# Last products by column halves in a hybrid decoder block with a mixture of experts

## The chip, the cores and the metric

The kernel runs on one core of one Trainium2 chip. The number is the device time of one execution in microseconds, as the median of several runs. The engines are TensorE (PE, with its weight loads shown as PEld), VectorE (DVE), ScalarE (ACT), GpSimd (POOL) and SyncE (SP), which issues most transfers. TensorE writes to PSUM, eight banks of 128 partitions by 512 float32 columns; everything else lies in SBUF or DRAM.

## The reference, cut to what matters

One layer: 512 tokens of 1024 features, a mixer (retention and dilated attention), then a mixture of experts with 4 of 32 experts for each token, and a last RMS norm.

```python
x = x + hybrid_mixer(rms_norm(x, norm_mix_g), w_in, w_out, pos)
...
logits = ht @ w_router + b_router
top_val, top_idx = lax.top_k(logits, TOP_K)          # 4 of 32
gates = softmax(top_val)
...
gu = xb @ w_gu + b_gu                                # 1024 -> 2048, one expert's rows
act = x_glu * sigmoid(1.702 * x_glu) * (x_lin + 1.0) # both clamped at 7
y[token] += gate * (act @ w_dn + b_dn)               # 1024 -> 1024
...
x = x + y
return x * rsqrt(mean(x * x, axis=-1) + 1e-5) * norm_final_g
```

The change concerns the last lines: the share of the last expert and of all down biases is added to x, and the final norm is taken.

## The kernel before

The 512 tokens lie as four chunks (`NC = 4`) of 128 rows; a row has 1024 columns, in two halves of `UW = 512`, since a PSUM bank holds 512. Each engine has its own written program; the order on an engine is the order of the code, and engines wait for each other through semaphores. There is no scheduler.

The experts run one after the other. For each, up to 128 rows of its tokens are gathered, multiplied with weights that stream in from DRAM (each float32 product is made of three products of a high and a low part), and the result is added to `acc_rows` in DRAM by a scatter. The residual x is in `acc_rows` too. The last expert is different: its result never goes through DRAM. ScalarE and VectorE split it by column halves into `y_hi` and `y_lo` (lines 1039 to 1042 and 1501 to 1506). Meanwhile, when the scatter of the expert before it is complete, SyncE loads the four chunks of `acc_rows` back into `x1` (line 520, one transfer of 512 KB for each chunk, semaphores `x_in[0]` to `x_in[3]`).

Then TensorE does what lines 2082 to 2093 say: for each chunk c and each half it adds three products in one PSUM bank: the gates times the down biases (`gateT`, `bdn`), and a matrix of zeros and ones that puts the expert's rows at their tokens (`hasT`) times `y_hi` and times `y_lo`. These are 4 x 2 x 3 = 24 products, all on line 2075. Chunk c uses banks `LAST_BANK[c]` and the one behind it, so 0 and 1, 2 and 3, 6 and 7, 4 and 5. The last expert's own result stands in banks 4 and 5, which is why chunk 3 waits for `y_lo`. After both halves of a chunk, `f_ps` goes up by one (it stands at 1 before, from line 2000).

Behind that, for each chunk:

- VectorE adds both banks to `x1` (`final_sum`, line 1545), waiting for the chunk's load and for `f_ps`, and signals `f_sum`.
- ScalarE squares the chunk and accumulates each row's sum of squares (`final_square`, line 1068), signals `f_sq`. The profile shows the write of the accumulator as an instruction of its own, ACTIVATION_READ_ACCUMULATOR.
- GpSimd multiplies chunks 0 and 1 by the gain (line 733).

With all four sums of squares, ScalarE takes the root (line 1081) beside VectorE's half variance (line 1553); four small VectorE steps on 128x4 numbers make the reciprocal root with one correction (lines 1556 to 1559); ScalarE scales chunks 0 and 1 (line 1075), VectorE chunks 2 and 3 (line 1562), and SyncE stores the four chunks (lines 543 and 545). Between the split and the last products every engine reads whether any expert had more rows than 128 and branches around the code for that case, which is not taken here.

Of the kernel before, what the change touches and what calls it, by code (L numbers as in the profile page):

```python
# [65 lines left out]
LAST_BANK = [0, 2, 6, 4]  # L66

# [88 lines left out]
def build(nc, x, norm_mix_g, w_in, w_out, norm_ffn_g, w_router, b_router,  # L156
# [299 lines left out]
    with block as block:  # L456
# [92 lines left out]
        def _(pl):  # L549
# [181 lines left out]
            for c in range(2):  # L731
                pl.wait_ge(f_sum, c + 1)
                nc.gpsimd.tensor_tensor(with_gain[:, c, :], x1[:, c, :], gain_row[:, :], ALU.mult).then_inc(f_gain, 1)

        @block.scalar
        def _(act_e):
# [328 lines left out]
            def final_square(c):  # L1065

                act_e.wait_ge(f_sum, c + 1)
                nc.scalar.activation((y, lin, sig, square_out)[c][:, :], x1[:, c, :], ACT.Square,
                                     accum_out=small[:, 10, c:c + 1]).then_inc(f_sq, 1)
# [8 lines left out]
            for c in range(NC):  # L1078
                final_square(c)
            act_e.wait_ge(f_sq, NC)  # L1080
# [6 lines left out]
        def _(v):  # L1087
# [453 lines left out]
            def final_sum(c):  # L1541

                v.wait_ge(x_in[c], 32)
                v.wait_ge(f_ps, c + 2)
                nc.vector.tensor_tensor(x1[:, c, :], x1[:, c, :], ps[:, LAST_BANK[c]:LAST_BANK[c] + 2, :].rearrange("p b t -> p (b t)"),
                                        ALU.add).then_inc(f_sum, 1)

            v.wait_ge(fin_g_in, 16)
            for c in range(NC):
                final_sum(c)  # L1550
            v.wait_ge(f_sq, NC)
            half_var, root, step, rstd = (small[:, k, 0:NC] for k in (11, 12, 13, 3))
            nc.vector.tensor_scalar(half_var, small[:, 10, 0:NC], -0.5 / D, -0.5 * EPS, ALU.mult, ALU.add).then_inc(f_var, 1)
            v.wait_ge(f_var, 1)
# [11 lines left out]
        def _(pe):  # L1566
# [515 lines left out]
            for c in range(NC):  # L2082
                for half in range(2):
                    if c == NC - 1:
                        pe.wait_ge(ylo_s, half + 1)
                    last_half(c, half, gateT, bdn, True, False)
                    if c == 0:
                        pe.wait_ge(yhi_s, half + 2)
                    last_half(c, half, hasT, y_hi, False, False)
                    if c == 0:  # L2090
                        pe.wait_ge(ylo_s, half + 1)
                    last = last_half(c, half, hasT, y_lo, False, True)
                last.then_inc(f_ps, 1)
# [22 lines left out]
```

## Time and profile before

| | |
|---|---|
| Median of 3 runs | 1419.56 us (1418.79 to 1420.21) |
| Span of the profiled execution | 1416.6 us |
| TensorE busy in it | 1389.3 us (98%), granted clock 0.996 |
| VectorE, ScalarE, GpSimd busy | 1246.5, 1055.2, 402.8 us |
| First of the last products, by the trace | 1398.3 us |
| First store issued | 1409.66 us |

The span runs from the first to the last instruction of one execution; the runs' time has some 3 us more around it. The experts fill almost the whole of it. All that the change touches lies in the last 20 us. Times in the rows below are counted from the span's start. A bracket at the end of a row says how long the engine had been idle before it, and what ended that. A row with x2 or x4 merges neighbours: its length runs from the first's start to the last's end.

### The profile page before, as it was taken

To read this page: it belongs to the slowest core of one execution; us is meant where nothing else is said; L and a number is where in the kernel's file an instruction comes from. 1 tells how busy PE (TensorE), PEld (TensorE's weight loads), DVE (VectorE), ACT (ScalarE), POOL (GpSimd) and SP (SyncE) were. 2 spreads that over 40 slices of the span, in tenths; PEclk is the share of its full clock that TensorE was granted. 3 is DMA by queue.
4 is the path that set the end of the run, shared out by engine and by line. 5 is a ranking of instruction groups with operands and counts; after the bars stand their busy time and mean duration, and the time that the engine had idled before them with its cause. 6 is when DMAs were issued, how large, how long until landed. Compare 5 with 4: busy or idle time off the path is not lost.

```text
span 1416.6 us, 19760 instructions
## 1 busy us (share of the span) xinstructions
PE 1389.3 (98%) x6583; PEld 1154.8 (82%) x6583; DVE 1246.5 (88%) x959; ACT 1055.2 (74%) x779; POOL 402.8 (28%) x233
## 2 busy tenths in 40 slices
PE   7999999999999999999999999999999999999996
PEld 6877888878888888888888888888888888888884
DVE  5534647499999999999999999999999999999996
ACT  5234334488888888888888888888888888888875
POOL 0000001067433333333333333333333333333332
PEclk9999999999999999999999999999999999999998
DMA  8311423389999999999999999999999999999993
GB/s 312 106 38 60 134 75 123 124 305 367 385 388 383 382 380 383 379 380 374 380 378 384 375 382 381 380 378 383 382 379 382 383 387 381 383 383 381 383 358 131
DMA packets 80135, 453.73 MB, mean 320 GB/s; under 512 B 12825, under 2 KB 13089, under 8 KB 31852
## 3 DMA queue, kind: packets, MB, share of 16 engines
q1 hardware_dynamic: 68968, 432.55, 77.5%
q0 software_dynamic: 10016, 17.44, 4.8%
q10 hardware_dynamic: 1124, 3.38, 0.7%
q8 instruction: 17, 0.28, 0.1%
q14 instruction: 10, 0.08, 0.0%
HBM read 447.60 MB, written 22.59 MB: 332 GB/s over the span
## 4 chain that ended last, share of the span: by engine, by line
PE 93%; DVE 4%; ACT 2%; DMA 1%; issue 1%; DVEq 0%; ACTq 0%
PE ps L1947 16%; PE ps L1952 16%; PE ps L1948 16%; PE ps L1905 8%; PE ps L1907 8%; PE ps L1913 8%; PE ps L1583 4%; PE ps L1584 4%; PE ps L1591 4%; PE ps L1896 2%; PE ps L1883 2%; DVE wlo L1103 1%; PE ps L1686 1%; DVE wlo L1112 1%; PE ps L1717 1%; PE ps L1667 1%
## 5 line engine op out<-in xcount | busy, mean ns | idle before, releaser
L1947 PE MATMUL ps<-whi,xT_hi 128*128 128x512 f32 x992 | 389.4, 393 | 1.7 <-ACT ps L959 1.0
L1948 PE MATMUL ps<-whi,xT_lo 128*128 128x512 f32 x992 | 386.1, 389 | 0.0
L1112 DVE TENSOR_TENSOR wlo<-raw,whi 128x2048 fp32r<-128x2048 f32 x138 | 315.9, 2293 | 45.6 <-ACT whi L752 45.3
L752 ACT ACTIVATE whi<-raw 128x2048 fp32r<-128x2048 f32 x138 | 264.9, 1920 | 90.2 <-PE ps L1952 71.3
L1108 DVE SCALAR_TENSOR_TENSOR wlo<-raw,gffn,whi 128x2048 fp32r<-128x2048 f32 x124 | 311.0, 2551 | 0.9
L1952 PE MATMUL ps<-wlo,xT_hi 128*128 128x512 f32 x992 | 265.6, 389 | 0.0
L750 ACT ACTIVATE whi<-raw,gffn 128x2048 fp32r<-128x2048 f32 x124 | 245.5, 2004 | 9.9 <-PE ps L1952 9.9
L1947 PEld LDWEIGHTS ps<-whi,xT_hi 128*128 128x128 f32 x992 | 186.4, 188 | 40.6 <-ACT ps L959 1.4
L1952 PEld LDWEIGHTS ps<-wlo,xT_hi 128*128 128x128 f32 x992 | 186.2, 188 | 38.6
L1948 PEld LDWEIGHTS ps<-whi,xT_lo 128*128 128x128 f32 x992 | 186.4, 188 | 37.7
L1905 PE MATMUL ps<-whi,actT_hi 128*128 128x512 f32 x496 | 195.9, 395 | 0.0
L1907 PE MATMUL ps<-whi,actT_lo 128*128 128x512 f32 x496 | 193.2, 390 | 0.0
L1108 DVE SCALAR_TENSOR_TENSOR wlo<-raw_b,gffn,whi 128x2048 fp32r<-128x2048 f32 x62 | 147.1, 2373 | 0.0
L1108 DVE SCALAR_TENSOR_TENSOR wlo<-raw_a,gffn,whi 128x2048 fp32r<-128x2048 f32 x62 | 145.2, 2342 | 0.0
L750 ACT ACTIVATE whi<-raw_a,gffn 128x2048 fp32r<-128x2048 f32 x62 | 124.6, 2010 | 22.0 <-PE ps L1952 22.0
L750 ACT ACTIVATE whi<-raw_b,gffn 128x2048 fp32r<-128x2048 f32 x62 | 124.5, 2008 | 21.9 <-PE ps L1952 21.9
L1913 PE MATMUL ps<-wlo,actT_hi 128*128 128x512 f32 x496 | 132.7, 389 | 0.0
L627 POOL COPY idx_scatter<-tab 128x1 uint32 (+1 forms) x31 | 50.6, 1632 | 286.1 <-ACT y L940 286.0
L627 POOL COPY idx_gather<-tab 128x1 uint32 (+1 forms) x30 | 13.5, 449 | 336.6 <-PE ps L1883 334.2
L1913 PEld LDWEIGHTS ps<-wlo,actT_hi 128*128 128x128 f32 x496 | 93.1, 188 | 19.7
L1907 PEld LDWEIGHTS ps<-whi,actT_lo 128*128 128x128 f32 x496 | 93.2, 188 | 18.4
L1905 PEld LDWEIGHTS ps<-whi,actT_hi 128*128 128x128 f32 x496 | 93.2, 188 | 18.3
(269 smaller groups left out, 1926.2 us busy)
## 6 DMA issues: line engine op xcount, KB each, us to landing
raw<-in_w_gate_up SPq DMA_DIRECT2D x130, 1024.0 KB, 8.6
raw<-in_w_down SPq DMA_DIRECT2D x126, 1024.0 KB, 9.1
raw_a<-in_w_gate_up SPq DMA_DIRECT2D x63, 1024.0 KB, 7.5
raw_b<-in_w_gate_up SPq DMA_DIRECT2D x63, 1024.0 KB, 8.0
raw<-in_w_in SPq DMA_DIRECT2D x14, 1024.0 KB, 5.2
raw<-in_w_out SPq DMA_DIRECT2D x4, 1024.0 KB, 5.0
x<-in_x SPq DMA_DIRECT2D x4, 512.0 KB, 7.4
acc_rows<-x SPq DMA_DIRECT2D x4, 512.0 KB, 5.3
```

What stands on the lines that cost most here:

```text
L627: return nc.gpsimd.tensor_copy(index[:, 0:1], tab[:, bass.ds(e, 1), 0].bitcast(U32))
L750: nc.scalar.activation(whi_slot(n), raw_slot(slot_of(n)), ACT.Copy, scale=gffn_of(n)).then_inc(hi_done, 1)
L752: nc.scalar.activation(whi_slot(n), raw_slot(slot_of(n)), ACT.Copy).then_inc(hi_done, 1)
L1108: nc.vector.scalar_tensor_tensor(out=wlo_slot(n), in0=raw_slot(slot_of(n)), scalar=gffn_of(n), in1=whi_slot(n).bitcast(F32), op0=ALU.mult, ...
L1112: nc.vector.tensor_tensor(wlo_slot(n), raw_slot(slot_of(n)), whi_slot(n).bitcast(F32), ALU.subtract).then_inc(lo_done, 1)
L1583: mm(out_ap, x_hi_of(k), w_hi_ap, start=opened and k == 0, stop=False)
L1905: mm(ps[:, bank + half, :], x_hi_t[:, k0 + k, :], w_hi_ap, start=k0 + k == 0 and not started, stop=False, skip_group_check=started)
L1907: mm(ps[:, bank + half, :], x_lo_t[:, k0 + k, :], w_hi_ap, start=False, stop=False, skip_group_check=started)
L1913: last = mm(ps[:, bank + half, :], x_hi_t[:, k0 + k, :], w_lo_ap, start=False, stop=k0 + k == KD - 1, skip_group_check=started)
L1947: mm(ps[:, part, :], xT_hi[:, u, :], w_hi_ap, start=False, stop=False, skip_group_check=True)
L1948: mm(ps[:, part, :], xT_lo[:, u, :], w_hi_ap, start=False, stop=False, skip_group_check=True)
L1952: last = mm(ps[:, part, :], xT_hi[:, u, :], w_lo_ap, start=False, stop=u == U_GU - 1, skip_group_check=True)
```

## The change

`LAST_HALVES` sets a new order of eight pieces, each a chunk and a column half: left halves of chunks 0, 1, 2, right halves of 0, 1, 2, then both halves of chunk 3. TensorE makes its three products for one piece after the other and signals `f_ps` after each. VectorE's sums, ScalarE's squares, `f_sum` and `f_sq` go by pieces in the same order. A row now has two sums of squares, in columns 0 to 3 and 4 to 7 of `small[:, 10]`; VectorE adds them in one more instruction of 128x4, for which the root and the half variance wait. GpSimd waits for a chunk's right half. Scalings and stores stay whole chunks.

```diff
--- before.py
+++ after.py
@@ -64,6 +64,7 @@
 U_ALL = U_MOE + E * U_E
 NOVER = 15
 LAST_BANK = [0, 2, 6, 4]
+LAST_HALVES = [(0, 0), (1, 0), (2, 0), (0, 1), (1, 1), (2, 1), (3, 0), (3, 1)]
 
 
 C_ID = 0
@@ -729,7 +730,7 @@
 
             pl.wait_ge(fin_g_in, 16)
             for c in range(2):
-                pl.wait_ge(f_sum, c + 1)
+                pl.wait_ge(f_sum, LAST_HALVES.index((c, 1)) + 1)
                 nc.gpsimd.tensor_tensor(with_gain[:, c, :], x1[:, c, :], gain_row[:, :], ALU.mult).then_inc(f_gain, 1)
 
         @block.scalar
@@ -1062,11 +1063,13 @@
 
             nc.scalar.activation(small[:, 12, 0:1], cst[:, C_ONE:C_ONE + 1], ACT.Sqrt)
 
-            def final_square(c):
-
-                act_e.wait_ge(f_sum, c + 1)
-                nc.scalar.activation((y, lin, sig, square_out)[c][:, :], x1[:, c, :], ACT.Square,
-                                     accum_out=small[:, 10, c:c + 1]).then_inc(f_sq, 1)
+            def final_square(k):
+
+                c, half = LAST_HALVES[k]
+                piece = slice(half * UW, (half + 1) * UW)
+                act_e.wait_ge(f_sum, k + 1)
+                nc.scalar.activation((y, lin, sig, square_out)[c][:, piece], x1[:, c, piece], ACT.Square,
+                                     accum_out=small[:, 10, half * NC + c:half * NC + c + 1]).then_inc(f_sq, 1)
 
             def final_scale(c):
 
@@ -1075,9 +1078,9 @@
                 nc.scalar.activation(with_gain[:, c, :], with_gain[:, c, :], ACT.Copy,
                                      scale=small[:, 3, c:c + 1]).then_inc(hn_s, 1)
 
-            for c in range(NC):
-                final_square(c)
-            act_e.wait_ge(f_sq, NC)
+            for k in range(2 * NC):
+                final_square(k)
+            act_e.wait_ge(f_var, 1)
             nc.scalar.activation(small[:, 12, 0:NC], small[:, 10, 0:NC], ACT.Sqrt, scale=1.0 / D,
                                  bias=cst[:, C_EPS:C_EPS + 1]).then_inc(f_root, 1)
             final_scale(0)
@@ -1538,20 +1541,23 @@
                                                     ALU.add).then_inc(v_add, 1)
 
 
-            def final_sum(c):
-
+            def final_sum(k):
+
+                c, half = LAST_HALVES[k]
+                piece = x1[:, c, half * UW:(half + 1) * UW]
                 v.wait_ge(x_in[c], 32)
-                v.wait_ge(f_ps, c + 2)
-                nc.vector.tensor_tensor(x1[:, c, :], x1[:, c, :], ps[:, LAST_BANK[c]:LAST_BANK[c] + 2, :].rearrange("p b t -> p (b t)"),
-                                        ALU.add).then_inc(f_sum, 1)
+                v.wait_ge(f_ps, k + 2)
+                nc.vector.tensor_tensor(piece, piece, ps[:, LAST_BANK[c] + half, :], ALU.add).then_inc(f_sum, 1)
 
             v.wait_ge(fin_g_in, 16)
-            for c in range(NC):
-                final_sum(c)
-            v.wait_ge(f_sq, NC)
+            for k in range(2 * NC):
+                final_sum(k)
+            v.wait_ge(f_sq, 2 * NC)
             half_var, root, step, rstd = (small[:, k, 0:NC] for k in (11, 12, 13, 3))
+            nc.vector.tensor_tensor(small[:, 10, 0:NC], small[:, 10, 0:NC], small[:, 10, NC:2 * NC], ALU.add).then_inc(f_var, 1)
+            v.wait_ge(f_var, 1)
             nc.vector.tensor_scalar(half_var, small[:, 10, 0:NC], -0.5 / D, -0.5 * EPS, ALU.mult, ALU.add).then_inc(f_var, 1)
-            v.wait_ge(f_var, 1)
+            v.wait_ge(f_var, 2)
             v.wait_ge(f_root, 1)
             link(nc.vector.reciprocal(root, root))
             link(nc.vector.tensor_tensor(step, root, root, ALU.mult))
@@ -2079,18 +2085,16 @@
             pe.wait_ge(bdn_s, 1)
             pe.wait_ge(bdn_zero, 1)
             pe.wait_ge(hasT_s, 1)
-            for c in range(NC):
-                for half in range(2):
-                    if c == NC - 1:
-                        pe.wait_ge(ylo_s, half + 1)
-                    last_half(c, half, gateT, bdn, True, False)
-                    if c == 0:
-                        pe.wait_ge(yhi_s, half + 2)
-                    last_half(c, half, hasT, y_hi, False, False)
-                    if c == 0:
-                        pe.wait_ge(ylo_s, half + 1)
-                    last = last_half(c, half, hasT, y_lo, False, True)
-                last.then_inc(f_ps, 1)
+            for c, half in LAST_HALVES:
+                if c == NC - 1:
+                    pe.wait_ge(ylo_s, half + 1)
+                last_half(c, half, gateT, bdn, True, False)
+                if c == 0:
+                    pe.wait_ge(yhi_s, half + 2)
+                last_half(c, half, hasT, y_hi, False, False)
+                if c == 0:
+                    pe.wait_ge(ylo_s, half + 1)
+                last_half(c, half, hasT, y_lo, False, True).then_inc(f_ps, 1)
 
 
 _INS = ["x", "norm_mix_g", "w_in", "w_out", "norm_ffn_g", "w_router", "b_router",
```

TensorE, the last products: first as they stood, then as they stand now. Three rows are one piece. The name `last_halves_read` is the semaphore of `y_hi`, `last_y_lo` that of `y_lo`.

```order
L2075 MATMUL ps<-bdn,gateT 128x512 [waits down_bias_cleared,hasT_ready,down_bias_ready,gateT_lo_ready]
L2075 MATMUL ps<-y_hi,hasT 128x512 [waits last_halves_read]
L2075 MATMUL ps<-y_lo,hasT 128x512 [waits last_y_lo]
L2075 MATMUL ps<-bdn,gateT 128x512
L2075 MATMUL ps<-y_hi,hasT 128x512 [waits last_halves_read]
L2075 MATMUL ps<-y_lo,hasT 128x512 [waits last_y_lo]
L2075 MATMUL ps<-bdn,gateT 128x512
```

```order
L2081 MATMUL ps<-y_hi,hasT 128x512 [waits last_halves_read]
L2081 MATMUL ps<-y_lo,hasT 128x512 [waits last_y_lo]
L2081 MATMUL ps<-bdn,gateT 128x512
L2081 MATMUL ps<-y_hi,hasT 128x512
L2081 MATMUL ps<-y_lo,hasT 128x512
L2081 MATMUL ps<-bdn,gateT 128x512
L2081 MATMUL ps<-y_hi,hasT 128x512
L2081 MATMUL ps<-y_lo,hasT 128x512
L2081 MATMUL ps<-bdn,gateT 128x512
L2081 MATMUL ps<-y_hi,hasT 128x512 [waits last_halves_read]
L2081 MATMUL ps<-y_lo,hasT 128x512 [waits last_y_lo]
```

Between the pair of waits for the left half of `y` and the pair for the right half there was one product, the first of the second piece; now there are seven.

VectorE, the sums and the steps behind them, before and now. `last_rows_summed` is `f_ps`, `x_in0` to `x_in3` are the loads of the chunks.

```order
L1545 TENSOR_TENSOR x_52<-x_52,ps 128x1024 [waits last_rows_summed,x_in0,final_gain_in]
L1545 TENSOR_TENSOR x_52<-x_52,ps 128x1024 [waits last_rows_summed,x_in1]
L1545 TENSOR_TENSOR x_52<-x_52,ps 128x1024 [waits last_rows_summed,x_in2]
L1545 TENSOR_TENSOR x_52<-x_52,ps 128x1024 [waits last_rows_summed,x_in3]
L1553 TENSOR_SCALAR small<-small 128x4 [waits final_squares]
L1556 RECIPROCAL small<-small 128x4 [waits final_root,final_variance]
```

```order
L1550 TENSOR_TENSOR x_52<-x_52,ps 128x512 [waits last_rows_summed,x_in0,final_gain_in]
L1550 TENSOR_TENSOR x_52<-x_52,ps 128x512 [waits last_rows_summed,x_in1]
L1550 TENSOR_TENSOR x_52<-x_52,ps 128x512 [waits last_rows_summed,x_in2]
L1550 TENSOR_TENSOR x_52<-x_52,ps 128x512 [waits last_rows_summed,x_in0]
L1550 TENSOR_TENSOR x_52<-x_52,ps 128x512 [waits last_rows_summed,x_in1]
L1550 TENSOR_TENSOR x_52<-x_52,ps 128x512 [waits last_rows_summed,x_in2]
L1550 TENSOR_TENSOR x_52<-x_52,ps 128x512 [waits last_rows_summed,x_in3] x2
L1557 TENSOR_TENSOR small<-small 128x4 [waits final_squares]
L1559 TENSOR_SCALAR small<-small 128x4 [waits final_variance]
L1562 RECIPROCAL small<-small 128x4 [waits final_root,final_variance]
```

The wait for the load of chunk 2 stood in front of the third of four whole sums, and stands in front of the third of eight half sums. The new addition stands between the squares and the half variance.

## Rows read from the trace of the kernel before

**Rows 1.** The chain that ended last, late part: start us, us, what.
```profile
1399.85 4.84 PE ps L2075 x20
...
1404.78 1.23 DVE x L1545
...
1406.03 1.16 ACT square_out L1068 x2
...
1407.22 0.31 ACT small L1081
```

**Rows 2.** Instructions in order of time, VectorE: start us, us, line, what.
```profile
1401.01 1.22 DVE L1545 TENSOR_TENSOR x<-x,ps 128x1024 f32<-128x1024 f32 x1 [0.99 <-DMA x<-acc_rows]
...
1402.15 1.21 DVE L1545 TENSOR_TENSOR x<-x,ps 128x1024 f32<-128x1024 f32 x1
...
1403.42 1.22 DVE L1545 TENSOR_TENSOR x<-x,ps 128x1024 f32<-128x1024 f32 x1
```

**Rows 3.** The same view, the queue of SyncE: loads of chunks 0 to 3.
```profile
1396.20 0.33 SPq L520 DMA_DIRECT2D x<-acc_rows  x1
...
1396.58 0.43 SPq L520 DMA_DIRECT2D x<-acc_rows  x1
...
1397.05 0.43 SPq L520 DMA_DIRECT2D x<-acc_rows  x1
...
1397.53 1.28 SPq L520 DMA_DIRECT2D x<-acc_rows  x1
```

**Rows 4.** Line L520: load 0; loads 0, 1; loads 1, 2; all four.
```profile
DMA to landing us min/median/max: 4.5/4.5/4.5
...
DMA to landing us min/median/max: 4.5/4.9/5.3
...
DMA to landing us min/median/max: 5.3/5.8/6.3
...
DMA to landing us min/median/max: 4.5/5.8/7.0
```

**Rows 5.** Busy time by stretch: stretch, length, busy by engine, PEclk, DMA share, GB/s.
```profile
1403.25:1403.50 0.25, 0.25 (x3) 0.21 (x2) 0.20 (x2) 0.25 (x3) 0.25 (x1) 1.00 0.04 16
```

**Rows 6.** DMA queues from 1397.5 to 1398: kind: packets, MB, share.
```profile
q8 instruction: 1, 0.02, 11.6%
```

**Rows 7.** Instructions in order of time, weight loads and VectorE: waits for y_lo.
```profile
1398.77 0.19 PEld L2075 LDWEIGHTS ps<-y_lo,hasT 128*128 128x128 f32 x1 [0.23 <-DVE y_lo L1504]
...
1399.27 0.75 DVE L1504 SCALAR_TENSOR_TENSOR y_lo<-ps,tab,y_hi 128x512 fp32r<-128x512 f32 x1 [0.55 <-ACT y_hi L1041]
...
1400.07 0.19 PEld L2075 LDWEIGHTS ps<-y_lo,hasT 128*128 128x128 f32 x1 [0.60 <-DVE y_lo L1504]
```

**Rows 8.** The same view, VectorE at 240 us: two half sums.
```profile
240.50 1.29 DVE L1285 TENSOR_TENSOR x<-x,ps 128x512 f32<-128x512 f32 x2
```

**Rows 9.** The same view, ScalarE: one square's read, the next square.
```profile
1403.24 0.18 ACT L1068 ACTIVATION_READ_ACCUMULATOR y<-x 128x1 f32 x1
...
1403.40 1.07 ACT L1068 ACTIVATE lin<-x 128x1024 f32<-128x1024 f32 x1
```

**Rows 10.** The same view, ScalarE at 249 us: a square of 512 columns.
```profile
248.95 0.62 ACT L877 ACTIVATE squares<-x 128x512 f32<-128x512 f32 x1
...
249.47 0.19 ACT L877 ACTIVATION_READ_ACCUMULATOR squares<-x 128x1 f32 x1
```

**Rows 11.** The same view, VectorE: small steps.
```profile
1407.83 0.16 DVE L1557 TENSOR_TENSOR small<-small 128x4 f32<-128x4 f32 x1
...
1408.03 0.16 DVE L1558 TENSOR_TENSOR small<-small 128x4 f32<-128x4 f32 x1
```

**Rows 12.** The same view, GpSimd and ScalarE: products with the gain, scalings.
```profile
1402.39 4.73 POOL L733 TENSOR_TENSOR with_gain<-x,gain_row 128x1024 f32<-128x1024 f32 x2 [9.81 <-DVE x L1545]
...
1408.48 2.19 ACT L1075 ACTIVATE with_gain<-with_gain,small 128x1024 f32<-128x1024 f32 x2 [0.96 <-DVE small L1559]
```

**Rows 13.** Busy time by stretch, as in rows 5: the stores.
```profile
1409.65:1416.50 6.85, 0.00 (x0) 0.00 (x0) 1.25 (x2) 1.02 (x1) 0.00 (x0) 0.50 0.77 306
```

## The prediction

> **What bounds the kernel now.** I read the chain of waits first [rows 1]. Behind the last expert it is TensorE's 24 last products, ending at 1404.68, then VectorE's sum of chunk 3, ScalarE's square of chunk 3, a root on four numbers, four small VectorE steps and the scaling. The stores follow. So the change sits on the chain of the last 20 us and touches nothing ahead of it: the span up to 1396 is the same program.
>
> The chain names TensorE, and here the reader has to look at who else was ready at the same moment. The four sums begin at 1401.01, 1402.15, 1403.42 [rows 2] and 1404.78 [rows 1], each 1.21 to 1.22 long. So VectorE is all but full: 5.00 us hold four sums of 4.88 in all. TensorE holds back the last two by 0.06 and 0.14 at most. A faster TensorE alone would give 0.2 us.
>
> The third party is the rows themselves. A sum adds products to a chunk that SyncE loads back from DRAM. The four loads are issued at 1396.20, 1396.58, 1397.05 and 1397.53 [rows 3]. They take 4.5, 5.3, 6.3 and 7.0 us to land [rows 4]; these rows are for the first load alone, the first two, the middle two and all four, and each maximum is the latest load's. That is 1400.7, 1401.9, 1403.35 and 1404.5. Each sum starts within 0.1 to 0.35 us of its own load's landing. Before the change loads and sums march in step, one chunk every 1.3 us, so the loads hide. One reason for the late landings shows: the 16 DMA engines together move only 16 GB/s from 1403.25 on, while load 3 is not there before 1404.5 [rows 5], so a few stragglers land last, and one fetch of instructions sits in the same queues at 1397.5 (11.6% of 16 engines over 0.5 us, so 0.93 us of one engine) [rows 6].
>
> **The change part by part.** I number the eight pieces in the new order: left halves of chunks 0, 1, 2, right halves of 0, 1, 2, then left and right of 3.
>
> TensorE keeps its 24 products. Before, it waited 0.23 us for the left y_lo, and 0.60 us for the right one inside chunk 0, which is complete at 1400.02 [rows 7]. In the new order six products (6 x 0.24 = 1.4 us; 20 took 4.84 [rows 1]) stand in front of the right half's waits, and TensorE arrives at them at about 1400.5, behind 1400.02. It gains some 0.7 us and ends at about 1404.0. That is a real gain, but nothing waits for it as long as VectorE or a load is later.
>
> VectorE gets eight sums of 128x512 for four of 128x1024. Two of just this kind, same tile and PSUM, took 1.29 us together [rows 8] against 1.21 to 1.22 for one whole: a half alone is 0.69, and back to back they stand 0.60 apart. Eight cost 7 x 0.60 + 0.69 = 4.9 us if nothing holds them: no gain and no loss. But the order of the loads they need is now 0, 1, 2, 0, 1, 2, 3, 3. The third piece needs chunk 2 after only two half sums of work. Piece 1 starts at 1401.01 as before and ends at 1401.70. Piece 2 waits for load 1 and runs 1402.1 to 1402.8. Piece 3 waits for load 2 and starts at 1403.42, where chunk 2's whole sum started, and ends at 1404.11. At that time the old order had two chunks summed and was well into the third; the new one has three halves, 1.5 chunks. Behind piece 3, in order on VectorE, stand pieces 4 to 6, whose data were there long ago, and 7 and 8. They run back to back: piece 8 starts at 1403.42 + 5 x 0.605 = 1406.44 and ends at 1407.13, against 1406.01 before.
>
> This is also the place to weigh the Trainium skill. The row shows overlap between neighbours (1.29 for two of 0.69). The Trainium skill, page VectorE: DVE Perf Modes, section on the TRN2 errata, says that memory latency is exposed between instructions and many small tiles pay it each; read strictly, pieces would stand 0.69 apart and piece 8 would end at 1407.56. ScalarE would then end about 0.1 us later than in my sum, so both readings lie in my range; the row is what I take.
>
> ScalarE gets eight squares for four, with eight reads of the accumulator. One whole: the next square stands 0.16 us behind the start of the read [rows 9]. A 512 wide one of an earlier stage has its read 0.52 behind its own start, and the read takes 0.19 [rows 10]. So halves stand 0.68 apart, and they are slower than VectorE's 0.60: ScalarE becomes the one that ends last. Square 3 starts at 1404.13, 0.02 behind its sum; square 8 at 1404.13 + 5 x 0.68 = 1407.53; its number is there at 1407.53 + 0.52 + 0.19 = 1408.24. Before it was 1406.03 + 1.16 = 1407.19 [rows 1]. That is **+1.05 us**. The intended saving (half a last square, 0.45 us) is in this sum already.
>
> The joining addition has the size of the small steps, which stand 0.20 apart [rows 11]. Before, root and half variance started together at 1407.22, and only the root was on the chain. Now the root waits for the addition, and crosses from VectorE to ScalarE: 0.20, at most 0.28. **+0.2 us**. The half variance, one more small step of 0.16, still hides beside the root (0.31).
>
> GpSimd multiplies chunks 0 and 1 by the gain, 4.73 us for both [rows 12]. It may start chunk 0 when piece 4 is summed (1404.7 instead of 1402.25) and ends at 1409.6. ScalarE scales both products in 2.19 us from 1408.48 on [rows 12], so it takes up the second at about 1409.6, and everything later by 1.25 at 1410.8 after. The cover of the second product shrinks from 2.4 to 1.2 us and is still there. Cost nothing; if a product took 0.6 us more each, it would begin to show.
>
> The stores leave from 1409.65 on and fill the DMA at 306 GB/s to the end [rows 13]: a shift of the scaling goes to the end one to one.
>
> Sum: 1.05 + 0.2 = +1.25 us. Span 1416.6 + 1.25 = 1417.8. The median of the runs is 1419.56, 3.0 us above the span; with the same surroundings the forecast is **1420.8 us**, 0.09% slower, which counts as no change: about 0.2% (2.84 us) is what a measurement of this kernel can tell, and the three runs before lie 1.4 us apart.
>
> **Rivals.** (A) *The loads are on time.* If the stragglers do not come in another build or execution, load 2 lands nearer to 1402, VectorE is never held, and ScalarE sets the end: square 1 at 1401.72 + 7 x 0.68 = 1406.48, done at 1407.19. That is exactly the old time, the addition makes it +0.2; if the first sum too starts up to 0.4 us earlier, -0.2. So 1419.4 to 1419.8. For it: the straggling is some 1.3 us behind the bulk. Against: all four landings of this trace show it, and the loads and the code ahead of them are unchanged. Chance 0.17.
>
> (B) *The saving comes as meant*, since TensorE is the bound that the chain names: TensorE earlier by 0.7 and last square shorter by 0.45, less 0.2 for the addition, gives -0.95: 1418.6. Against it: VectorE was full and had at most 0.2 us from TensorE. Chance 0.04; even this is within 0.2%.
>
> (C) *Slower than measurable: instructions come late.* VectorE and ScalarE have a dozen more instructions in the tail. If this moves the end of a fetched block into the squares while the loads fill the queues, the engine stands for a fetch: 0.93 us of one DMA engine [rows 6], behind loads that are up to 1.4 us late. 1.25 + 2.3 = +3.6: 1423.1. It decides from 1.6 us of standing on. The Trainium skill, Runtime: NRT & Kernel Launch, section Instruction fetch mechanics, says that crossing a block is mostly hidden; no run here shows a crossing in the tail. Chance 0.04.
>
> (D) *GpSimd's cover is gone*: products slower beside VectorE's halves, +1.3 to +2.5 us, 1421 to 1422. Before, both products ran beside VectorE's sums at 2.4 us each, so 0.04. That the program doesn't do what it says is excluded by the order of its instructions; 0.
>
> **The numbers.** Forecast 0.71 (1420.3 to 1421.4: the addition 0.2 to 0.28, piece spacing 0.60 to 0.69, landing of load 2 give or take 0.3), A 0.17, B 0.04, C 0.04, D 0.04. Predicted 1420.8. The range takes in A and D's lower part, with half a microsecond of the median's own scatter: 1419.2 to 1421.9. Chances: faster by over 0.2% 0.01, slower by over 0.2% 0.04, within 0.95.
>
> **What would show it.** Right: TensorE ends at about 1404.0; the third sum waits for a DMA landing, with VectorE idle about 0.4 and 0.6 us ahead of pieces 2 and 3; sums 4 to 8 without gaps; squares 0.68 apart without waits from the third on; root some 0.2 us behind the addition; stores leaving at 1410.9. Wrong: load 2 landing before 1402.3, idle time of ScalarE between the late squares, GpSimd waited for by a scaling, or any difference ahead of 1396.

## The result and the profile after

| | before | changed |
|---|---|---|
| Median of 21 runs each, in turn on one chip | 1418.91 us | 1420.95 us |
| Lowest and highest | 1416.8, 1421.84 | 1418.97, 1422.88 |
| Span of the profiled execution | 1416.6 us | 1418.1 us |
| Ratio | | 1.0015, 95% interval 1.0009 to 1.0020 |

The changed kernel is 2.1 us slower by the ratio (1.3 to 2.8). That is inside the forecast range; 21 runs tell it from no difference, and the upper end of the interval just reaches the 0.2% that was set as the limit. But the forecast sum was 1.25 us, and the trace shows that what lies behind the measured number is in good part something else than the reason given. In the traces the place of the tail in the span shifts by up to 3 us with what happened before it, so I count from two marks: the first sum of x, and the start of VectorE's second `y_lo`.

The late part of the chain of waits of the changed kernel (start, length in us, what):

```profile
1396.21 6.30 DMA x<-acc_rows
1402.52 0.02 issue
1402.54 0.70 DVE x L1550
1403.23 0.02 issue
1403.26 0.72 ACT sig L1071 x2
...
1405.82 1.23 ACT square_out L1071 x4
1407.05 0.02 issue
1407.08 1.61 DVE small L1557
1408.68 0.03 issue
1408.71 0.30 ACT small L1084
```

TensorE has left the chain [rows 1]. It now begins with the load of chunk 2, as forecast, and goes on through the squares. Then stands something that was not forecast at all: the joining addition, four numbers per row, takes 1.61 us. The same stretch in order of time, VectorE, ScalarE and GpSimd:

```profile
1400.34 0.69 DVE L1550 TENSOR_TENSOR x<-x,ps 128x512 f32<-128x512 f32 x1 [1.00 <-DMA x<-acc_rows]
1401.21 0.69 DVE L1550 TENSOR_TENSOR x<-x,ps 128x512 f32<-128x512 f32 x1 [0.18 <-DMA x<-acc_rows]
1402.54 3.68 DVE L1550 TENSOR_TENSOR x<-x,ps 128x512 f32<-128x512 f32 x6 [0.64 <-DMA x<-acc_rows]
...
1403.98 4.67 POOL L734 TENSOR_TENSOR with_gain<-x,gain_row 128x1024 f32<-128x1024 f32 x2 [12.08 <-DVE x L1550]
...
1404.50 0.61 ACT L1071 ACTIVATE lin<-x 128x512 f32<-128x512 f32 x1
1405.02 0.18 ACT L1071 ACTIVATION_READ_ACCUMULATOR lin<-x 128x1 f32 x1
1405.12 0.61 ACT L1071 ACTIVATE sig<-x 128x512 f32<-128x512 f32 x1
...
1407.08 1.60 DVE L1557 TENSOR_TENSOR small<-small 128x4 f32<-128x4 f32 x1 [0.86 <-ACT square_out L1071]
1408.71 0.17 DVE L1559 TENSOR_SCALAR small<-small 128x4 f32<-128x4 f32 x1
```

Three readings. The sums [rows 2] stand much as forecast: held 0.18 and 0.64 us by the loads of chunks 1 and 2, then six in 3.68 us without a gap. The squares are 0.62 apart, not 0.68. And the addition ends at 1408.68, just behind GpSimd's second product, which ends at 1403.98 + 4.67 = 1408.65. Before, that product ended at 1402.39 + 4.73 = 1407.12 [rows 12], and VectorE's first small step began at 1407.22, 0.1 us later: the program had a deadline there that no wait in it expresses and no bracket shows.

The bracket of the first sum names the load of chunk 0. But in eight of the thirteen traces here, these two among them, the first sum starts 1.74 or 1.75 us behind the start of the second `y_lo`, while the load lands 0.1 to 0.4 us ahead of it. What stands there is then more likely VectorE's own way through the branch; no run tests it. The third sum starts 0.03 us behind the landing of its load (1396.21 + 6.30 = 1402.51).

From the first sum: the root started 6.21 us behind it before and 8.37 behind it now. Of these 2.16 us, 0.53 lie ahead of the addition (square 8 complete 6.71 behind the first sum, against 6.18), and 1.63 are the addition.

### The profile page after: what moved, and what is told of

The parts are those of the page before. It is cut to its first block, busy times and chain, and to the rows that moved or that the text cites. A ratio compares the mean times of both kernels' runs of the same rounds, so it can differ in the third digit from the quotient of the medians.

```text
span 1418.1 us, 19777 instructions
## 1 busy us (share of the span) xinstructions
PE 1388.6 (98%) x6583; PEld 1154.3 (81%) x6583; DVE 1248.3 (88%) x964; ACT 1055.2 (74%) x787; POOL 402.3 (28%) x233
## 4 chain that ended last, share of the span: by engine, by line
PE 92%; DVE 3%; DMA 2%; ACT 2%; issue 1%; DVEq 0%; ACTq 0%; SPq 0%; POOLq 0%
PE ps L1953 16%; PE ps L1958 16%; PE ps L1954 16%; PE ps L1911 8%; PE ps L1913 8%; PE ps L1919 8%; PE ps L1589 4%; PE ps L1590 4%; PE ps L1597 4%; PE ps L1902 2%; PE ps L1889 2%; DVE wlo L1106 1%; PE ps L1692 1%; PE ps L1723 1%; PE ps L1673 1%
```

## The experiments

Theory S: a VectorE instruction that needs what GpSimd is using to reach SBUF stands until GpSimd's instruction is done, and the new order moved GpSimd's products into VectorE's small steps. What the runs can show is who stands and until when; that the way to SBUF is the reason stays theory. Rivals: the joining step is dear by itself (J); only the hold by the load of chunk 2 counts (L).

All times of one comparison come from the same chip. The last two columns are the start of VectorE's scaling in the one profiled execution, counted from the start of the second `y_lo` and from the first sum. They differ by what the first sum waited; in e1, e5 and e8 to e10 that was TensorE.

| kernel | ratio to before, 95% interval | scaling behind y_lo | behind the first sum |
|---|---|---|---|
| before | 1 | 9.15 us | 7.41 us |
| changed | 1.0015, 1.0009 to 1.0020 | 11.32 | 9.57 |
| e1, before with GpSimd late | 1.0013, 1.0004 to 1.0022 | 11.76 | 9.58 |
| e2, changed, no products with the gain | 1.0004, 0.9995 to 1.0013 | 10.07 | 8.32 |
| e3, changed, chunk order | 0.9999, 0.9990 to 1.0008 | 9.31 | 7.56 |
| e4, changed, join by reduction | 1.0012, 1.0003 to 1.0021 | 11.04 | 9.29 |
| e5, only chunk 3 halved | 1.0001, 0.9992 to 1.0010 | 10.43 | 7.75 |
| e6, changed, products in quarters | 1.0013, 1.0004 to 1.0022 | 11.24 | 9.49 |
| e7, changed, two chunks then two | 1.0003, 0.9994 to 1.0012 | 10.25 | 8.50 |
| e8, before, stream shifted | 1.0003, 0.9993 to 1.0012 | 13.11 | 7.89 |
| e9, changed, stream shifted | 1.0019, 1.0010 to 1.0028 | 11.44 | 9.41 |
| e10, e5, stream shifted | 1.0011, 1.0002 to 1.0021 | 10.35 | 7.74 |
| e11, changed, products by pieces | 1.0000, 0.9990 to 1.0009 | 10.09 | 8.34 |

**e1: GpSimd late in the kernel before.**

```diff
-                pl.wait_ge(f_sum, c + 1)
+                pl.wait_ge(f_sum, c + 3)
```

> The kernel before, with one number changed: GpSimd's two products with the gain wait for the third and the fourth whole sum instead of the first and the second. Sums, squares, root and VectorE's small steps are those of before. Theory S (shared access to SBUF): a VectorE instruction whose two operands both lie in SBUF stands until GpSimd's product is done. The products then run from about 1404.8 to 1409.5, the square of the root (line 1557, 0.16 us before, at 1407.8) lasts until the second product ends, so 1.5 to 1.7 us, half variance and reciprocal (one operand) stay at 0.17 and 0.18, and the end is 1.4 to 1.6 us later than before (ratio 1.0010 to 1.0011). Rival J (the joining addition itself is dear, as the first reader of the two sets of sums): there is no joining addition here, the step stays 0.16 us, the time that of before.

Measured 1.0013. In order of time:

```profile
1405.24 4.65 POOL L733 TENSOR_TENSOR with_gain<-x,gain_row 128x1024 f32<-128x1024 f32 x2 [12.90 <-DVE x L1545]
...
1407.66 2.26 DVE L1553 TENSOR_SCALAR small<-small 128x4 f32<-128x4 f32 x1 [1.22 <-ACT square_out L1068]
1407.66 0.30 ACT L1081 ACTIVATE small<-small,cst 128x4 f32<-128x4 f32 x1
1409.95 0.18 DVE L1556 RECIPROCAL small<-small 128x4 f32<-128x4 f32 x1
```

No halves, no joining step, one number changed, and from the first sum to the scaling the kernel before now takes 9.58 us, like the changed one (9.57). So J is not needed for a step to stand. The size came out larger than expected (9.58 - 7.41 = 2.2 us in the trace, 0.3 of them sums that waited for TensorE; 1.4 to 1.6 forecast), and the wrong instruction stood. I had expected the half variance to pass, since it has one operand; it took 2.26 us, to 1409.92, when GpSimd ended at 1409.89. So two operands are not the condition.

**e2: no products.** The products of chunks 0 and 1 with the gain are left out, so these rows come out without the gain.

```diff
-            for c in range(2):
-                pl.wait_ge(f_sum, LAST_HALVES.index((c, 1)) + 1)
-                nc.gpsimd.tensor_tensor(with_gain[:, c, :], x1[:, c, :], gain_row[:, :], ALU.mult).then_inc(f_gain, 1)
...
-                act_e.wait_ge(f_gain, c + 1)
...
-                nc.scalar.activation(with_gain[:, c, :], with_gain[:, c, :], ACT.Copy,
+                nc.scalar.activation(with_gain[:, c, :], x1[:, c, :], ACT.Copy,
```

> The changed kernel without GpSimd's products with the gain of chunks 0 and 1: that multiplication is left out, ScalarE scales x1 straight into with_gain. Theory S: the joining addition falls from 1.60 to 0.16-0.20 us, the end lies 1.4 us ahead of the changed kernel, so 0.5 to 0.8 us behind before (ratio 1.0004 to 1.0006). Rival J: the addition stays near 1.6 us and the time stays that of the changed kernel (1.0015).

```profile
1402.63 3.68 DVE L1546 TENSOR_TENSOR x<-x,ps 128x512 f32<-128x512 f32 x6 [0.56 <-DMA x<-acc_rows]
...
1407.18 0.16 DVE L1553 TENSOR_TENSOR small<-small 128x4 f32<-128x4 f32 x1 [0.87 <-ACT square_out L1068]
```

The same addition in the same place takes 0.16 us, so J falls, and 1.0004 is what was expected. The hold by the load stays, 0.56 us.

**e3: chunk order.**

```diff
-LAST_HALVES = [(0, 0), (1, 0), (2, 0), (0, 1), (1, 1), (2, 1), (3, 0), (3, 1)]
+LAST_HALVES = [(0, 0), (0, 1), (1, 0), (1, 1), (2, 0), (2, 1), (3, 0), (3, 1)]
```

> The changed kernel with the list LAST_HALVES in chunk order (left and right of 0, of 1, of 2, of 3); halves, signals and joining addition stay. Theory S with L (the order holds VectorE at the load of chunk 2 and moves GpSimd's start): no idle time of 0.6 us ahead of the third piece, sums end where they ended before, last square about 0.5 us earlier than before relative to the first sum, GpSimd starts after the second piece and ends some 4.8 us later, the addition stands only 0.3-0.5 us for it, and the root starts within 0.1 us of where it did before: the time is that of before (ratio 0.9998 to 1.0002). Rival J: addition 1.6 us, root 1.1 us late, ratio 1.0008. Rival P (VectorE was never held, halving costs by itself): as the changed kernel, 1.0015.

```profile
1400.26 5.37 DVE L1550 TENSOR_TENSOR x<-x,ps 128x512 f32<-128x512 f32 x8 [1.00 <-DMA x<-acc_rows]
...
1401.70 4.74 POOL L734 TENSOR_TENSOR with_gain<-x,gain_row 128x1024 f32<-128x1024 f32 x2 [9.86 <-DVE x L1550]
...
1406.42 0.17 DVE L1557 TENSOR_TENSOR small<-small 128x4 f32<-128x4 f32 x1 [0.79 <-ACT square_out L1071]
```

Halves, signals and joining addition are all there, and the time is that of before. No sum waits for a load behind the first. The eight take 5.37 us, not the 4.9 of VectorE's own pace: they stand 0.67 apart on average, which is about what TensorE needs for three products of 0.23. So the last square is complete 6.13 us behind the first sum (6.18 before), and not 0.5 us sooner as I had expected. GpSimd is through at 1406.44, when the addition starts at 1406.42. So the price of the change lies in the order of the eight pieces, which sets both the hold and GpSimd's start, and not in the halving, which costs 0.15 us here (7.56 against 7.41).

**e4: join with one operand.**

```diff
-            nc.vector.tensor_tensor(small[:, 10, 0:NC], small[:, 10, 0:NC], small[:, 10, NC:2 * NC], ALU.add).then_inc(f_var, 1)
+            nc.vector.tensor_reduce(out=small[:, 14, 0:NC], in_=small[:, 10, 0:2 * NC].rearrange("p (h c) -> p c h", h=2),
+                                    op=ALU.add, axis=AX.X).then_inc(f_var, 1)
```

> The changed kernel with the joining step as a reduction over a 4x2 view, one operand, in place of an addition of two operands. Theory S: the join takes 0.16-0.20 us beside GpSimd's product, then half variance, root and reciprocal run, and now the square of the root (two operands) stands until the second product is done, about 0.5 us. The end lies 0.6-0.7 us ahead of the changed kernel, 1.3-1.5 us behind before (ratio 1.0010). Rival J: the join is dear in any form, 1.6 us, time as changed; or, if only this one addition is dear, the whole 1.4 us come back (ratio 1.0005) and no later step is long.

```profile
1405.72 4.65 POOL L734 TENSOR_TENSOR with_gain<-x,gain_row 128x1024 f32<-128x1024 f32 x2 [12.18 <-DVE x L1550]
...
1408.83 0.16 DVE L1557 TENSOR_REDUCE small<-small 128x4 f32<-128x8 f32 x1 [0.87 <-ACT square_out L1071]
1409.02 1.39 DVE L1560 TENSOR_SCALAR small<-small 128x4 f32<-128x4 f32 x1
```

The reduction passes beside GpSimd in 0.16 us, so a join is not dear in this form. The half variance behind it stands 1.39 us, to 1410.41 (GpSimd: 1410.37). The stand has moved one step back, past the root's start, and the reciprocal behind it on VectorE is late again. Gain against the changed kernel: 0.3 us by either of the last two columns, where I had expected 0.6 to 0.7.

e1 and e4 together give the condition as these traces show it: TENSOR_TENSOR with both operands in SBUF and TENSOR_SCALAR from SBUF to SBUF stand, TENSOR_REDUCE does not, nor do the sums of x with one operand in PSUM, which ran beside GpSimd all along. The Trainium skill, GPSIMD Engine Reference, section Specifications, has this rule: GpSimd's interfaces to SBUF are shared with VectorE, with contention from VectorE instructions that have two SBUF inputs or are in a 2-port performance mode. The traces agree, with 1.60 us for the first kind and 2.26 for TENSOR_SCALAR, if that ran in such a mode, which no row shows.

**e5: only chunk 3 by halves.** Sums and squares of chunks 0 to 2 are whole and the order is by chunk; the two sums of chunk 3's rows are joined by a reduction.

```diff
-LAST_HALVES = [(0, 0), (1, 0), (2, 0), (0, 1), (1, 1), (2, 1), (3, 0), (3, 1)]
+PIECES = [(0, 0, 2), (1, 0, 2), (2, 0, 2), (3, 0, 1), (3, 1, 1)]      # chunk, first half, halves
...
-                pl.wait_ge(f_sum, LAST_HALVES.index((c, 1)) + 1)
+                pl.wait_ge(f_sum, c + 1)
```

> Sums and squares of chunks 0, 1 and 2 whole, in chunk order, as in the kernel before; only chunk 3 by halves; the two sums of its rows are joined by a reduction (one operand, 128x1). GpSimd starts behind chunk 0's whole sum, as before. Theory S (a VectorE instruction that needs the second access to SBUF, by two operands or as TENSOR_SCALAR, stands until GpSimd's running product ends): last square done 0.5 us earlier than before relative to the first sum, join 0.2, root 0.3 us earlier than before; GpSimd's second product ends about 0.1-0.2 us behind the join, so the half variance stands that long, hidden beside the root. End 0.2-0.3 us ahead of before, ratio 0.9997 to 1.0000, which the runs can't tell from 1; in the trace the first small step stands under 0.4 us. Rival T (the stand has another cause, a halved square or a joining step as such): a step of 1.4-1.6 us shows here too, ratio 1.0008.

```profile
1403.15 5.11 DVE L1550 TENSOR_TENSOR x<-x,ps 128x1024 f32<-128x1024 f32 x5 [1.93 <-PE ps L2082]
```

1.0001, and no step stands (reduction 0.15, half variance 0.17): rival T falls. GpSimd was through at 1409.25, 0.26 us ahead of the reduction. The forecast gain did not come: from the first sum to the scaling it takes 7.75 us (7.41 before). Two gaps of 0.12 and 0.14 us between the sums are waits for TensorE, and the first sum itself waited 1.93 us for TensorE; e8 to e10 are on this. The 0.5 us expected of the last square were not there either: ScalarE runs through its last three squares without a gap (1407.10 to 1409.48), so without the waits it would have been some 0.1 us ahead of before (an estimate from its squares of 1.06 and 0.61 us).

**e6: GpSimd's products in quarters.**

```diff
-                nc.gpsimd.tensor_tensor(with_gain[:, c, :], x1[:, c, :], gain_row[:, :], ALU.mult).then_inc(f_gain, 1)
+                for q in range(4):
+                    part = slice(q * 256, (q + 1) * 256)
+                    last = nc.gpsimd.tensor_tensor(with_gain[:, c, part], x1[:, c, part], gain_row[:, part], ALU.mult)
+                last.then_inc(f_gain, 1)
```

> The changed kernel with each of GpSimd's two products with the gain in four instructions of 256 columns (about 0.6 us each) in place of one of 2.4 us; their start and sum are the same. Theory S1 (VectorE stands until the GpSimd instruction that is running ends): the addition stands at most 0.7 us, and each later small step with two operands, and the TENSOR_SCALAR, may stand up to 0.6 us again, until GpSimd is through: the steps are spread, the root starts 0.9-1.5 us earlier than in the changed kernel, the sum of all stands is at most 1.6. Ratio 1.0005 to 1.0012. S2 (VectorE stands until GpSimd has nothing more to do): one stand of 1.4-1.8 us at the addition as in the changed kernel, ratio 1.0015.

```profile
1402.96 5.53 POOL L736 TENSOR_TENSOR with_gain<-x,gain_row 128x256 f32<-128x256 f32 x8 [12.11 <-DVE x L1553]
...
1406.06 0.41 DVE L1560 TENSOR_TENSOR small<-small 128x4 f32<-128x4 f32 x1 [0.87 <-ACT square_out L1074]
1406.50 0.66 DVE L1562 TENSOR_SCALAR small<-small 128x4 f32<-128x4 f32 x1
...
1407.19 0.18 DVE L1565 RECIPROCAL small<-small 128x4 f32<-128x4 f32 x1
1407.40 0.43 DVE L1566 TENSOR_TENSOR small<-small 128x4 f32<-128x4 f32 x1
1407.87 0.65 DVE L1567 TENSOR_TENSOR small<-small 128x4 f32<-128x4 f32 x1
1408.54 0.16 DVE L1568 SCALAR_TENSOR_TENSOR small<-small 128x4 f32<-128x4 f32 x1
```

S1, clearly: VectorE gets in when one GpSimd instruction ends, and stands again at the next step. Four stands make 0.25 + 0.49 + 0.27 + 0.49 = 1.5 us, the products take 5.53 in place of 4.67, and nothing is won. RECIPROCAL passes, like the reduction. Behind GpSimd's end at 1408.49 the last step is 0.16 again.

**e7: two chunks, then two.**

```diff
+LAST_HALVES = [(0, 0), (1, 0), (0, 1), (1, 1), (2, 0), (2, 1), (3, 0), (3, 1)]
```

> The changed kernel with the list in the order left of 0, left of 1, right of 0, right of 1, left and right of 2, left and right of 3. The load of chunk 2 is needed only by the fifth piece, and GpSimd starts behind the third. Theory S: no idle time of VectorE ahead of the third piece by a load; GpSimd starts 1.2 us after the second piece's start plus 0.7, so about 2.0-2.6 us behind the first sum (3.6 in the changed kernel, 1.4 in chunk order), ends 4.7 us later, and the addition, due 6.2-6.3 us behind the first sum, stands 0.4-1.1 us; the end lies 0.6-1.2 us ahead of the changed kernel: ratio 1.0003 to 1.0009, between chunk order (0.9999) and the changed kernel (1.0015). Rival L (the load's hold is the price, GpSimd's start is not): as chunk order, 0.9999, no stand.

```profile
1401.63 4.65 DVE L1550 TENSOR_TENSOR x<-x,ps 128x512 f32<-128x512 f32 x7 [0.39 <-DMA x<-acc_rows]
...
1403.07 4.72 POOL L734 TENSOR_TENSOR with_gain<-x,gain_row 128x1024 f32<-128x1024 f32 x2 [10.95 <-DVE x L1550]
...
1407.07 0.75 DVE L1557 TENSOR_TENSOR small<-small 128x4 f32<-128x4 f32 x1 [0.79 <-ACT square_out L1071]
```

No hold by load 2, and still a stand: 0.75 us, to 1407.82, with GpSimd through at 1407.79. L alone would have shown none. With GpSimd's start 1.4, 2.5 and 3.6 us behind the first sum (e3, e7, changed) the addition takes 0.17, 0.75 and 1.60.

**e11: products by pieces.** The changed kernel, its order untouched; GpSimd's two products become four, and start sooner.

```diff
-            for c in range(2):
-                pl.wait_ge(f_sum, LAST_HALVES.index((c, 1)) + 1)
+            for c, half in ((0, 0), (1, 0), (0, 1), (1, 1)):
+                piece = slice(half * UW, (half + 1) * UW)
+                pl.wait_ge(f_sum, LAST_HALVES.index((c, half)) + 1)
```

> The changed kernel, order and all, with GpSimd's two products with the gain in four of 512 columns, each waiting only for its own piece: left of 0, left of 1, right of 0, right of 1. Theory S: what costs is where GpSimd's work ends, not the order of the pieces as such. The left halves (1.2 us each) run beside pieces 1 to 3, the right halves start behind piece 4 at the soonest, 3.6 us behind the first sum, and end at about 6.0 to 6.2 us behind it; the joining addition is due at 6.7. So it takes 0.16-0.20 us in place of 1.60, the root starts 1.4 us earlier than in the changed kernel and the time is that of the kernel without the products: ratio 1.0003 to 1.0007. Rival: the addition stands although GpSimd is through, or products of 512 columns take over 1.5 us each beside VectorE: ratio 1.0010 or more.

```profile
1404.00 2.53 POOL L735 TENSOR_TENSOR with_gain<-x,gain_row 128x512 f32<-128x512 f32 x2 [0.37 <-DVE x L1553]
...
1407.18 0.16 DVE L1560 TENSOR_TENSOR small<-small 128x4 f32<-128x4 f32 x1 [0.87 <-ACT square_out L1074]
```

GpSimd ends at 1406.53 in place of 1408.65 in the changed kernel, the addition takes 0.16, and the ratio is 1.0000 (0.9990 to 1.0009). Both last columns are 1.2 us below the changed kernel, and 8.34 us is what the kernel without the products has (8.32). The ratio is better than the 1.0003 to 1.0007 expected. But it does not show that the order is free: its interval is 1.3 us wide to either side, and in the traces this order still takes 0.9 us more than before (8.34 against 7.41) and 0.8 more than chunk order (7.56). That is the hold by the loads.

**e8 to e10: TensorE's idle time.** In every trace up to here TensorE stands ahead of the fifth of the last products with no releaser shown: 0.34 us before, 1.21 in the changed kernel, 1.20 in e1, whose TensorE program is that of before. The three kernels have twenty products more in the branch that is not taken:

```diff
             with pe.If(total > 0):
+                pe.wait_ge(hasT_s, 1)
+                for _ in range(20):
+                    nc.tensor.transpose(ps[:, 2, 0:P], has[:, 0, :].bitcast(F32), ident)
```

> The kernel before with twenty more TensorE products in the branch that is not taken, ahead of the last products: nothing more is executed, only the place of what follows in the stream of instructions moves. In every trace so far TensorE stands 0.3 to 1.7 us ahead of the fifth last product with no releaser shown. Theory F: this is a block of instructions that arrives late, its fetch being the one seen among the loads of x; with the border moved off, TensorE has no such idle time, the last product ends 0.3-1.4 us earlier relative to y_lo, VectorE's sums are bound by VectorE and the loads: root 0.2-0.9 us earlier, ratio 0.9993 to 0.9999. If the fetch is also what makes the loads late (F2), the loads land in 3.3 to 5.7 us in place of 4.5 to 7.0. Rival G: the idle time comes from the matrix itself (banks, weights, waits): it stays at the fifth product.

> The changed kernel with the same twenty unexecuted products. F: no idle time ahead of the fifth product; this alone gains nothing, since VectorE waits for loads. F2: the load of chunk 2 lands about 1.3 us earlier relative to its issue, VectorE's idle time ahead of pieces 2 and 3 (0.18 and 0.64 us) falls under 0.2 in all, GpSimd starts and ends about 0.6-0.8 us earlier and the joining addition, 0.3-0.6 earlier, stands 1.3-1.6 us: end 0.5-0.8 us ahead of the changed kernel, ratio 1.0008 to 1.0012. F without F2: 1.0015. Theory S is untouched: the addition still stands to the end of GpSimd's second product.

> Only chunk 3 by halves, as before in this study, with the twenty unexecuted products. F: its first sum waited 1.9 us for TensorE; without the idle time it starts as in the kernel before, root 0.3 us earlier than in the padded kernel before if GpSimd's second product is through by then, else about the same; the half variance may stand up to 0.5 us. Ratio 0.9990 to 0.9997. G: as before padding, 1.0001.

TensorE around the last products, in the changed kernel, then in e8 and in e9:

```profile
1400.04 0.39 PE L2081 MATMUL ps<-y_hi,hasT 128*128 128x512 f32 x1 [1.21 <-issue]
```

```profile
1402.22 0.77 PE L2078 MATMUL ps<-bdn,gateT 128*128 128x512 f32 x1 [2.94 <-issue]
```

```profile
1401.02 0.47 PE L2084 MATMUL ps<-bdn,gateT 128*128 128x512 f32 x1 [1.72 <-issue]
```

The idle time moved, with nothing executed that was not executed before: from the fifth product to the first, in all three. Rival G falls, it belongs to the place in the stream of instructions. But the gain that F forecast did not come: what TensorE waits for is not sooner there, it is needed four products sooner. The kernels are no faster (1.0003, 1.0019, 1.0011; the intervals of the last two lie above 1, and for e10 its trace, much like e5's, gives no reason).

What it waits for can be narrowed down. One fetch of 16 KB on queue 8 runs among the loads of x in every one of the thirteen traces; in e5 from 1400 to 1401 the queues hold

```profile
q8 instruction: 1, 0.02, 5.8%
```

The times of its packet, and of TensorE's next product behind the idle time, in us:

| | fetch ends | TensorE goes on | between | idle |
|---|---|---|---|---|
| before | 1398.43 | 1399.85 | 1.42 | 0.34 |
| changed | 1398.74 | 1400.04 | 1.30 | 1.21 |
| e5 | 1400.99 | 1402.40 | 1.41 | 1.69 |
| e8 | 1400.50 | 1402.22 | 1.72 | 2.94 |
| e9 | 1399.29 | 1401.02 | 1.73 | 1.72 |

In the ten kernels without the twenty products the distance is 1.25 to 1.53 us, in the three with them 1.72 to 1.73, while the idle time itself goes from 0.34 to 2.94: it is as long as the fetch is late. That speaks for F. A releaser is shown in no trace, and what makes the fetch late stays open.

In e8's profiled execution, the slowest of its 11 (1423.09 us), the 2.94 us had a second price. The granted clock was 1.00 (2.4 GHz) until then, and 0.50 (1.2 GHz) behind it, here from 1402.5 to 1405:

```profile
1402.50:1405.00 2.50, 2.50 (x7) 1.92 (x7) 0.00 (x0) 0.00 (x0) 0.00 (x0) 0.50 0.39 154
```

Products started 0.43 us apart in that stretch (1402.79, 1403.21) and 0.23 from 1405.6 on, at 1.00 again. So the first sum waited 4.47 us for TensorE. The median of the 11 runs is 0.2 us below that of before, so one execution must differ much from another here. Behind the 1.72 us of e9 the clock stayed at 1.00.

F2 is not borne out, and not excluded: load 0 landed in 3.2 and 3.4 us in e5 and e8, where the fetch came latest, and in 4.5 to 4.8 elsewhere, but the slowest load took 7.0 to 7.2 us in every trace, and the hold by load 2 is still 0.63 us in e9. In e9 the addition stands 1.60 us again.

## Why the prediction was right or wrong

*TensorE is not the bound.* Right in what followed, wrong in its number: I had it end at 1404.0, 0.7 us sooner. It ended at 1404.34 + 0.39 = 1404.73, which is 6.1 us behind the second `y_lo` where it had been 5.4 (1404.68 - 1399.27): 0.7 us later, since the idle time ahead of its fifth product was 1.21 us. In the changed kernel this is hidden, since the pieces wait for loads.

*The load of chunk 2 holds VectorE.* Right. The load took 6.3 us, as before. I had pieces 2 and 3 wait 0.4 and 0.6 us, the trace has 0.18 and 0.64; piece 3 starts 2.20 us behind the first sum (2.41 forecast), and the rest runs through in 3.68 (3.71). In chunk order the hold is gone (e3).

*ScalarE's squares, +1.05.* The mechanism was right, the size was twice the real one: +0.53. Of the 0.52 too much, 0.21 is that piece 3 started sooner than forecast, and 0.31 is the spacing of the five squares behind it. The spacing of 0.68 had a term of 0.16 between the read of the accumulator and the next square [rows 9]. That was not ScalarE's own time but a wait: the second sum ended at 1402.15 + 1.21 = 1403.36 [rows 2], and the square began at 1403.40. Where no sum is waited for, the gap is 0.10 (1405.02 to 1405.12), squares are 0.62 apart, and VectorE's 0.60 is nearly as slow. A gap between two instructions is the engine's price only when nothing that the second waits for ends in it.

*The joining addition, +0.2.* This is the step that failed. It kept the root back by 1.63 us: 0.16 for itself (e2, e11), 0.03 to the root, and 1.44 in which it stood for GpSimd's product.

*GpSimd's later start costs nothing.* The same failure seen from the other side. I had compared its end with the next reader of its output, ScalarE's scaling, and found 1.2 us of cover; the forecast end (8.6 us behind the first sum, 8.31 measured) was near enough. But another engine needed not its output but that it be through, 0.1 us behind GpSimd's old end; that this is for its access to SBUF is theory S. Rival D had the right engine, a chance of 0.04 and the wrong direction: it had GpSimd slowed by VectorE. GpSimd's products took 4.67 us beside the halves, 4.73 before; VectorE was the one that stood.

*The sum.* 0.53 + 1.63 = 2.16 by the trace, 2.1 by the runs, 1.25 forecast: an overcharged term of 0.5 partly covered for a missing one of 1.4. That is one stroke of luck: without the overcharge the forecast would have been 0.7. The other is that the kernel before had a median of 1418.91 in this comparison and not the 1419.56 on which the forecast stands: 1420.95 is 0.15 us from the forecast 1420.8, the difference of the two kernels 0.8 to 0.9 from the forecast 1.25. Rivals A and B are out: the slowest load took 7.0 to 7.2 us in every trace, and the saving did not come. Rival C is not what happened in the tail of VectorE or ScalarE, though TensorE did stand for its place in the stream (e8 to e10).

By the traces (last column), the 2.16 us of the change are about 0.15 for halving and joining (e3), 0.8 for the order, by the loads (e11 against e3), and 1.2 for GpSimd's product (e11 against the changed kernel; the addition stood 1.44, but in e11 the loads held 0.2 us more). No kernel here is measurably faster than before. e3, e5 and e11 equal it within 0.1%.

## What to carry to other kernels

When a change moves the start of an engine's work, look not only at who reads its result, but at who runs beside it: in these traces a short VectorE TENSOR_TENSOR with two SBUF operands, or a TENSOR_SCALAR, stood until the GpSimd product that was under way was done, and the profile showed that as the step's own length, not as a wait. So a step of 0.16 us that takes 1.6 is the sign to look for. In an engine that works in order, a list that asks for its inputs 0, 1, 2 before it uses up 0 runs at the pace of the inputs; put the pieces in the order in which they land. And a bracket that names a releaser is to be compared with other traces: a distance that never changes points at the engine itself.

## What the hardware showed that I had not expected

- TENSOR_REDUCE (0.16 us, e4) and RECIPROCAL (0.18, e6) passed beside a running GpSimd product, TENSOR_TENSOR and TENSOR_SCALAR on 128x4 numbers did not (up to 1.60 and 2.26 us). Smaller GpSimd instructions shared out the stand without shortening it (1.5 us in four parts, e6).
- TensorE stood 0.34 to 1.72 us, in one trace 2.94, at a place that moved with the unexecuted instructions ahead of it, and went on 1.25 to 1.73 us behind the end of a fetch that runs among the loads of x in all thirteen traces. That it waits for just this fetch is likely by these distances, not shown by a releaser. That the fetch makes the loads late is not shown.
- After the 2.94 us the granted clock was 0.50 for some 3 us, and products started 0.43 us apart; after 1.72 us it stayed at 1.00 (e8, e9).
